# First MLP products with a 512-column matmul for both operand halves, and the cross sums added on VectorE

## The reference

```
for layer in range(2):
    h = rms_norm(x, norm_mix_g[layer])
    x = x + (attention mixer if layer == 0 else retention mixer)(h)
    h = rms_norm(x, norm_ffn_g[layer])
    x = x + square(relu(h @ ffn_w_in[layer])) @ ffn_w_out[layer]
return rms_norm(x, final_g)
```

## Time and profile before

| | |
|---|---|
| median of 3 runs | 1252.53 us (1252.07 to 1252.89) |
| span of the profiled execution | 1250.5 us, some 2 us under the median, for what lies around the span; the profile gives no other time of its own |
| PE busy | 1240.2 us, 99% |
| DVE busy | 932.1 us, 75% |
| ACT busy | 768.3 us, 61% |
| granted PE clock, mean | 0.998 of full |

### The profile page before, as it was taken

One profiled execution on the slowest core, in us unless ns is written; L12 is line 12 of the kernel. 1 busy time (PEld: TensorE's weight loads), 2 busy tenths in 40 slices (PEclk: granted clock), 3 DMA queues, 4 the chain that ended last, 5 costly groups with the idle time before them and its releaser, 6 DMA issues.

```text
span 1250.5 us, 19374 instructions
## 1 busy us (share of the span) xinstructions
PE 1240.2 (99%) x7446; PEld 1096.0 (88%) x7446; DVE 932.1 (75%) x1196; ACT 768.3 (61%) x1064; POOL 297.0 (24%) x330
## 2 busy tenths in 40 slices
PE   9999999999999999999999999999999999999997
PEld 6788888898998989989898889898889899898996
DVE  6588647599679596798666797567898957859578
ACT  6688755477564575665656645456667647456474
POOL 2343653111211112101131212231221122111220
PEclk9999999999999999999999999999999999999999
DMA  7357567778988989874968597879589899898992
GB/s 243 100 135 162 135 151 193 203 208 192 222 222 217 234 184 221 218 221 109 228 135 190 137 230 177 210 160 227 104 219 243 210 207 222 217 233 200 207 216 99
DMA packets 147980, 238.95 MB, mean 191 GB/s; under 512 B 51105, under 2 KB 72873, under 8 KB 147889
## 3 DMA queue, kind: packets, MB, share of 16 engines
q0 software_dynamic: 32352, 102.79, 43.7%
q1 hardware_dynamic: 115232, 134.60, 34.1%
q10 hardware_dynamic: 304, 0.33, 0.1%
HBM read 127.57 MB, written 2.11 MB: 104 GB/s over the span
## 4 chain that ended last, share of the span: by engine, by line
PE 96%; DMA 1%; DVE 1%; issue 0%; ACT 0%; SPq 0%; POOLq 0%; POOL 0%; DVEq 0%; ACTq 0%
PE bank L946 22%; PE bank L978 18%; PE bank L1353 11%; PE bank L1144 8%; PE bank L1421 6%; PE pv L978 5%; PE bank L1303 5%; PE pv L946 4%; PE bank L1084 4%; PE bank L1245 2%; PE bank L1111 2%; PE bank L1317 1%; PE pv L1060 1%; PE bank L1367 1%; PE pv L1367 1%; PE pv L1353 1%
## 5 line engine op out<-in xcount | busy, mean ns | idle before, releaser
L2225 DVE TENSOR_TENSOR w<-raw_tiles,w 128x1024 fp32r<-128x1024 f32 x312 | 371.3, 1220 | 90.2 <-ACT w L1563 90.0
L1563 ACT ACTIVATE w<-raw_tiles 128x1024 fp32r<-128x1024 f32 x312 | 315.2, 1051 | 122.7 <-PE bank L978 59.7
L3178 POOL DMA_DIRECT2D raw_tiles<-raw_tiles x176 | 152.3, 907 | 629.2 <-DVE w L2225 415.0
L946 PE MATMUL bank<-h_ops,w 128*128 128x256 f32 x2304 | 281.4, 283 | 0.0
L946 PEld LDWEIGHTS bank<-h_ops,w 128*128 128x128 f32 x2304 | 278.9, 192 | 0.7
L978 PE MATMUL bank<-w,arena_q 128*128 128x512 f32 x1044 | 241.3, 389 | 0.0
L978 PEld LDWEIGHTS bank<-w,arena_q 128*128 128x128 f32 x1044 | 195.3, 188 | 40.2
L1353 PE MATMUL bank<-w,h_ops 128*128 128x512 f32 x624 | 144.0, 390 | 0.0
L1353 PEld LDWEIGHTS bank<-w,h_ops 128*128 128x128 f32 x624 | 116.6, 188 | 23.9
L1144 PE MATMUL bank<-hT_hi,w 128*128 128x512 f32 x224 | 77.8, 397 | 0.0
L1645 ACT ACTIVATE arena_q<-arena 128x1024 fp32r<-128x1024 f32 x40 | 42.5, 1062 | 46.6 <-PE pv L978 19.8
(11 more groups left out here) (268 smaller groups left out, 1814.8 us busy)
## 6 DMA issues: line engine op xcount, KB each, us to landing
raw_tiles<-raw_tiles POOLq DMA_DIRECT2D x176, 512.0 KB, 5.5
raw_tiles<-in_ffn_w_in SPq DMA_DIRECT2D x64, 512.0 KB, 6.1
raw_tiles<-in_ffn_w_out SPq DMA_DIRECT2D x64, 512.0 KB, 6.1
raw_tiles<-in_odd_w_in SPq DMA_DIRECT2D x32, 512.0 KB, 5.5
raw_tiles<-in_even_w_in SPq DMA_DIRECT2D x48, 256.0 KB, 3.2
raw_tiles<-in_odd_w_in SPq DMA_DIRECT2D x32, 256.0 KB, 5.4
raw_tiles<-in_odd_w_out SPq DMA_DIRECT2D x16, 512.0 KB, 5.9
raw_tiles<-raw_tiles POOLq DMA_DIRECT2D x20, 256.0 KB, 4.3
```

The costliest lines, as they stand in the source:

```text
L946: mm = pe.matmul(bank[first + b][:, 256 * m:256 * m + 256], w_slots[use_slot(use)][:, p, k, c:c + P], h_ops[:, H_BLOCK[op], q, k, :], star ...
L1563: nc.scalar.activation(w_flat(use_slot(use), 0, half), raws[tile][:, 1024 * half:1024 * half + 1024], ACT.Copy).then_inc(m_hi, 1)
L2225: nc.vector.tensor_tensor(w_flat(use_slot(use), 1, half), raws[use_tile(key)][:, 1024 * half:1024 * half + 1024], w_flat(use_slot(use), 0, ...
L3178: pool.dma_start(raws[dst][:, part], raws[src][:, part], accum_op=ALU.add).then_inc(t_made[value][half], 16)
```

## The change

In the six chunks g = 1, 2, 3, 5, 6, 7 the first stage runs `wide_first_stage` in place of `first_stage`. For six of the seven products (all but product 5) the two matmuls with hi weights become one of 512 columns, whose moving operand is the hi and the lo half of the operand side by side; the one with lo weights stays at 256 columns and accumulates on the first half of the bank. A bank now holds the main sum (columns 0 to 255, LOW) and the cross sum (256 to 511, HIGH) of one m, so a product takes four banks: X is banks 2, 3 and 6, 7, Z is banks 4, 5 and 0, 1. Products 1, 2 and 3 all use Z, products 0, 4, 5 and 6 use X.

DVE's queue in a wide chunk (the lines marked + are new or moved; each `wide_` call is one operation over 128x512 that reads PSUM):

```
 w_lo_both(stage, 2)
+wide_cross(g, 0, 0)
+wide_cross(g, 0, 1)
 w_lo_both(stage, 3)
+wide_z(g, 0)
+wide_z_cross(g, 0)
+wide_z(g, 1)
+wide_z_cross(g, 1)
 w_lo_both(stage, 4)
+wide_cross(g, 1, 0)
+wide_cross(g, 1, 1)
 w_lo_both(stage, 5)
+wide_cross(g, 2, 0)
+wide_cross(g, 2, 1)
 w_lo_both(stage, 6)
+for b in range(2):
+    wide_x_cross(g, LOW, b)
+    wide_x_cross(g, HIGH, b)
+    wide_x(g, LOW, b)
 w_lo_both(stage + 1, 0)
+wide_x(g, HIGH, 0)
+wide_x(g, HIGH, 1)
 hidden_operand_sum(g, S1)
 operand_lo(g, 0)
 operand_lo(g, 1)
 hidden_operand_sum(g, S2)
+wide_last(g, 0)
 w_lo_both(stage + 1, 1)
+wide_last(g, 1)
 operand_lo(g, 2)
```

ACT's queue behind `operand_hi(g, 1)`:

```
-w_hi(stage + 1, 1, 0)
-relu_last(g, 0)
-w_hi(stage + 1, 1, 1)
-relu_last(g, 1)
+last_copy(g, 0)
+w_hi(stage + 1, 1, 0)
+last_copy(g, 1)
+w_hi(stage + 1, 1, 1)
+relu_last(g, 0)
+relu_last(g, 1)
 square(g, 3)
 operand_hi(g, 2)
```

with the new functions for the block of product 6:

```
+def last_copy(g, b):
+    act.wait_ge(p_done, use_done(first_use(g, 6), b))
+    act.wait_ge(a_lo, 7 * g)
+    nc.scalar.activation(hidden_part(0, b, HIGH), wide_part(6, b, LOW), ACT.Copy).then_inc(last_copied, 1)
+def wide_last(g, b):
+    v = hidden_part(0, b, HIGH)
+    dve.wait_ge(last_copied, wide_count(g) + b + 1)
+    nc.vector.tensor_tensor(v, v, wide_part(6, b, HIGH), ALU.add).then_inc(last_sum, 1)
 def relu_last(g, b):
+    if g % CHUNKS:
+        act.wait_ge(last_sum, wide_count(g) + b + 1)
+        v = hidden_part(0, b, HIGH)
+        nc.scalar.activation(v, v, ACT.Relu).then_inc(last_relu, 1)
+        return
```

More of the change, by code:

```diff
@@ L261, with wide_bank, wide_count @@
 FIRST_X, FIRST_Z, FIRST_Y = 2, 0, 4
+WIDE_X, WIDE_Z = (2, 6), (4, 0)
+WIDE = (0, 1, 2, 3, 4, 6)
+def wide_bank(i, b):
+    return (WIDE_Z if i in (1, 2, 3) else WIDE_X)[b]
+def wide_count(g):
+    return 2 * (g - g // CHUNKS - 1)
 OUT_BANK = (0, 2, 4, 2, 0, 0, 0)
@@ L664, in trunk @@
         last_relu = sem("last_relu")
+        z_added = sem("z_added")
+        low_cross = sem("low_cross")
+        high_cross = sem("high_cross")
+        last_copied = sem("last_copied")
+        last_sum = sem("last_sum")
+        cross_added = [sem(f"cross_added{n}") for n in range(3)]
         m_square = sem("m_square")
@@ L950, in first_stage, with wide_first_stage @@
                     mm.then_inc(p_done, 1)
+            def wide_first_stage(g, i):
+                use = first_use(g, i)
+                op, value = FIRST[i]
+                for b in range(2):
+                    if i == 0:
+                        pe.wait_ge(last_relu, 2 * g)
+                        if b == 1:
+                            pe.wait_ge(p_added, added(g - 1, 2))
+                    elif i == 1:
+                        pe.wait_ge(p_added, added(g - 1, 3 if b == 0 else 6))
+                    elif i == 2:
+                        pe.wait_ge(h_summed, 6 * g + b + 1)
+                    elif i == 3:
+                        pe.wait_ge(cross_added[1], wide_count(g) + b + 1)
+                    elif i == 4:
+                        pe.wait_ge(cross_added[0], wide_count(g) + b + 1)
+                    else:
+                        pe.wait_ge(h_summed, 6 * g + 2 * (i - 4) + b + 1)
+                    for m in range(2):
+                        dst = bank[wide_bank(i, b) + m]
+                        c = P * (2 * b + m)
+                        for k in range(4):
+                            if b == 0 and m == 0 and k % 2 == 0:
+                                pe.wait_ge(m_lo, 2 * use + k // 2 + 1)
+                            if i in WIDE:
[5 more added lines that the diff above has]
+                                               start=False, stop=(k == 3), skip_group_check=True)
+                            else:
+                                for n, (p, q) in enumerate(PASSES):
+                                    mm = pe.matmul(dst[:, 0:256], w_slots[use_slot(use)][:, p, k, c:c + P],
+                                                   h_ops[:, H_BLOCK[op], q, k, :],
+                                                   start=False, stop=(k == 3 and n == 2), skip_group_check=True)
+                    mm.then_inc(p_done, 1)
             def second_stage(g, i, t, turned=None):
@@ L2568, in mlp @@
                     w_lo(stage, 6, 1)
[L2569 to L2575, removed]
+                    w_lo_both(stage + 1, 0)
+                    hidden_sum(g, 2, 0)
+                    hidden_sum(g, 2, 1)
                 hidden_operand_sum(g, S1)
@@ L2578, in mlp @@
                 operand_lo(g, 1)
-                hidden_operand_sum(g, S2)
-                w_lo_both(stage + 1, 1)
+                if g % CHUNKS:
+                    hidden_operand_sum(g, S2)
+                    wide_last(g, 0)
+                    w_lo_both(stage + 1, 1)
+                    wide_last(g, 1)
+                else:
+                    hidden_operand_sum(g, S2)
+                    w_lo_both(stage + 1, 1)
                 if g % CHUNKS == 0:
```

57 lines of the change are left out of this document (47 added, 10 removed).

## The result

| | before | changed |
|---|---|---|
| median of 4 executions | 1252.3 us (1251.77 to 1252.89) | 1275.24 us (1274.25 to 1275.71) |
| ratio | | 1.0182, 95% interval 1.0171 to 1.0194 |
| span of the profiled execution | 1250.5 us | 1273.9 us (its own time 1275.71) |
| mean granted clock | 0.998 | 0.993 |

What follows compares the result with a forecast made beforehand. PE was taken to bound the kernel with DVE right behind. Five chunks at +3.15 us (15.8) and the last at 2.7 gave 18.5 over the median, 1271.0 us; range 1262 to 1281.

Steps and rivals of the forecast that it cites:

- What bounds the kernel: Both stages: PE busy throughout, DVE right behind it; PE's margin at the second stage's product 6 is 0.33 us.
- The saving of 7.7 us: First-stage matmuls: each triple falls from 360.0 to 346.7 ns, 1.28 us per chunk, 7.7 us in six chunks.
- The first stage's waits: PE waits for DVE: 0.12 us at product 2, 0.14 at 3, 0.54 at 5, 0.09 at the second stage's start.
- The stage change and the second stage: DVE's `operand_lo(2)` 3.66 us late; PE stands 2.2 us at product 2, about 1.3 more later; chunk +3.15.
- DMA: Next stage's loads move 3.7 us later with 1.1 us of cover; POOL's sums have the same cover or more.
- rival 1: PE's clock falls after each chunk's 2.2 us gap: 9 us more, 1280 us, or 1289 at twice that; chance 0.08.
- Rival 2: Second stage: only product 2 stalls, DVE catches up before product 6; 1.9 us per chunk, 1264 us; chance 0.10.
- Rival 3: Second stage: DVE's lateness never reaches PE, so the kernel gets faster, 1244.9 to 1250.3 us; chance 0.10.
- Rival 4: First stage: the 512-column matmul runs as two; +2 us, counted within the first case, no chance of its own.
- The sum on the span: Whole kernel: five chunks at 3.15 us and the last at 2.7 add 18.5 to the span of 1250.5, giving 1269.0.
- the last chunk: Second stage there has one `w_lo` fewer ahead of `add_product(5, 0)`: costs 2.0 to 3.15 us, 2.7 taken.
- the likeliest case: Whole kernel: 1271.0 us, own range 1266 to 1277; 1276 if first-stage stalls are twice as long; chance 0.72.

Runs made afterwards that it cites:

- Experiment 2: Kernel before plus only product 6's detour (ACT copy, one DVE operation per half, then ACT's ReLU), all matmuls old: 1274.06 us, ratio 1.0177.
- both-512 run: Changed kernel with the second matmul of each pair also 512 columns wide (lo weights on both operand halves): 1318.21 us.
- experiment 4: Changed kernel with both last sums ahead of S2 and DVE's first stage reordered, `w_lo` of 3, 4 and 6 split into halves: 1254.18 us, ratio 1.0014.
- Experiments 1 to 3: 1: changed kernel without product 6's copy and last sums, 1252.22 us. 2: see Experiment 2. 3: changed kernel, last sums ahead of S2, 1258.26 us.
- the filled gap: Changed kernel with eight unread 512-column matmuls put in PE's gap ahead of the second stage's product 2: 1274.61 us, ratio 1.0180.
- experiment 10: Changed kernel with only products 1, 2, 3 wide, product 6's ReLU from PSUM, `w_lo(3)` and `w_lo(4)` in halves: 1250.32 us, ratio 0.9987 to the kernel before.
- four and four: Changed kernel with each m's matmuls grouped by width, four of 512 columns and then four of 256: 1273.91 us.

## Why the prediction was right, point by point

**What bounds the kernel: right.** PE is busy throughout, and DVE finishes the addition that product 6 waits for 0.33 us before PE needs it. Experiment 2, which changes no matmul, shows that what is added beyond the slack is paid in full: against the chunk's start `operand_lo(2)` is 4.0 us later there (372.32 - 323.36 against 368.64 - 323.69), less 0.33 of margin and 0.18 of gap is 3.5, and chunk 2's second stage, where the clock stayed, took 41.59 us against 38.11, 3.48 more.

**The saving of 7.7 us: too large.** I took the upper bound, 346.7 ns a pair; over a stage it is 353.3, so a triple saves 6.7 ns, not 13.3: 576 x 6.7 = 3.9 us. My reason, the same count of elements, holds for a stream of one width only (the both-512 run) and not for a mix. By the Trainium skill's figure (TensorE: Matmul & The Clock Gate, Back-to-back issue gap) 2.5 ns a triple would be saved; the mix lies between that and the rows' 13.3.

**The first stage's waits: right in kind, in part in size.** Product 5 waited as forecast: 0.54 late was forecast, and experiment 4, which takes the wait away, shortens the stage by 0.42. The gaps at products 2 and 3 don't show in chunk 1. By the numbers the slower pairs gave DVE the 0.1 us that it lacked: 16 pairs a product, each 6 ns longer, bring PE to product 2 0.2 us later than forecast. Stage 1 of chunk 1 took 40.08 us in place of 40.31, 0.23 less, where 0.39 was forecast; the smaller saving on the pairs and the smaller waits partly cancel.

**The stage change and the second stage: right.** `operand_lo(2)` 372.30 forecast, 372.29 measured; product 2's first matmul 376.74 and 376.71, each 0.2 later than forecast when counted from the chunk's own, earlier start. Chunk 1's second stage took 3.6 us longer; 3.54 was forecast (3.15 + 0.39). The parts that I named for the 3.66 of `operand_lo(2)`, 1.2 + 2.9 - 0.33, add up to 3.77: the kernel before had DVE standing for 0.12 us there too (366.17 + 2.35 against 368.64). Experiments 1 to 3 show that it is mostly the position: the same operations ahead of S2 cost 6 us in the whole kernel in place of 23.

**DMA: wrong in one place.** I gave POOL's sums "the same cover or more". In chunk 2 that did not hold. From the chain and ACT's timeline of the changed kernel:

```profile
410.30 9.98 DMA raw_tiles<-raw_tiles
```

```profile
420.36 1.06 ACT L1633 ACTIVATE w<-raw_tiles 128x1024 fp32r<-128x1024 f32 x1 [1.09 <-DMA raw_tiles<-raw_tiles]
```

A sum by DMA takes 5.6 us in the median on the page of this run; this one took 10.0, the second half of `w_hi(4)` waited for it, and product 3 waited 1.0 us for the `wide_cross` queued behind `w_lo(4)`. It happened in chunks 2 and 6. Their first stages took 1.2 and 0.7 us more than chunk 1's. Why the sum was late is open. That the loads, shifted by DVE's lateness, fell on it would be a reading, but the runs speak against it as the whole cause: the detour alone (experiment 2) shifts them by as much, and in its chunk 2 ACT did not wait for that sum at all; in experiments 3 and 4 `operand_lo(2)` is only 0.9 and 0.4 us late, and there ACT waited for it, 1.1 and 1.0 us.

**Rivals.** The clock (rival 1) came true in four chunks, at the level and length assumed, but not at its price of 9 us: stage 2 took 4.0 us more than before in those chunks against 3.6 in chunk 1, so some 1.7 us in all; the filled gap gave back 0.6 of the median, within the spread. The four executions of the changed kernel don't show even that: their mean granted clocks were 0.993, 0.998, 0.990 and 0.993, their times 1275.71, 1275.48, 1275.00 and 1274.25 us, and the one whose clock was that of the kernel before was not the fastest; with a spread of 1.5 us they can't settle 1.7. Rival 2 (only product 2 stalls) is excluded by the chunks' lengths and the further waits of L1045 for `add_product`. Rival 3 (faster) needed the chain behind `wide_last(1)` off the path; it was on it. Rival 4 (the 512 runs as two) is excluded: in the both-512 run such a matmul takes 226.7 ns.

**The sum on the span:** 18.5 forecast, 23.4 measured. The difference of 4.9 is 1.9 for the late sums (1.2 + 0.7), 1.7 for the clock, 0.9 for the first stages (0.15 x 6) and 0.5 for the last chunk, which I had put at 2.7 and whose second stage cost as much as the others', less some 0.2 that this execution was ahead at chunk 1. The pace lay within the bounds that I had drawn; the late sums stood in no term, and the clock only in a rival. The first three have one sign, and 1275.24 still falls under the 1276 of the likeliest case because its bounds were wide enough, not because they named the late sums. That part is luck.

## What to carry to other kernels

Where an engine runs right behind the bound one, walk both in-order queues operation by operation: 1.2 us of DVE work per chunk cost 3.5 to 3.6, because a sum was put behind two long operations and another engine's chain behind the sum. A split result that has to be joined wants its join where an engine has slack and nothing serial behind it; take the wide form only for the products whose join falls there (experiment 10). A pace read from a stream of one width doesn't carry over to a mix of widths.

## What the runs showed of the hardware that was not expected

- Matmuls of 512 and 256 columns in turn take 352.5 ns a pair in product 0 and 353.3 over a stage, where the uniform streams give 226.7 + 120.0 = 346.7 ns; four and four, 349 to 350.6. Neither the pieces of the moving operand nor which tile moves changes it (352.5 ns in both runs).
- A PE gap of 2.0 us was followed by some 3.4 us at the 1.2 GHz level in four chunks of six (0.53 and 0.58 granted over the 3.4 us windows shown) and by nothing in two, with gaps of the same length. The Trainium skill (TensorE: Matmul & The Clock Gate, The HAM clock gate) says that idleness closes the gate; the four chunks agree. It is not the place in the program that decides: in experiment 2, with gaps of the same 2.0 us, the clock fell in chunks 1, 5, 6 and 7 and stayed in 2 and 3. What decides is open.
